# A decoder layer on one core: the first modulation loaded and computed by column halves, with v's first weights in between

## What is computed

```
sh1, sc1, ... = split(silu(c) @ w_ada + b_ada, 6)          # c: 9 rows (prompt and 8 samples), 1024 wide
h = x * rsqrt(mean(x*x) + eps) * norm1_g * (1 + sc1) + sh1
z = h @ w_in                                                # q, k, v, u, v (for the gating), gates
```

## Time and profile before

| | us |
|---|---|
| median of 3 runs | 1307.18 (1304.03 to 1307.71) |
| profiled execution, device time | 1306.45 |
| its span, first to last instruction | 1304.8 |
| PE busy in the span | 1230.2 (94%) |
| DVE, ACT, POOL busy | 659.8, 545.2, 195.6 |

### The profile page before, as it was taken

How to read it: one execution, slowest core, us unless ns; L and a number is a source line. 1 busy time by engine, 2 the same in 40 slices (tenths; PEclk the granted TensorE clock), 3 DMA queues, 4 the chain that set the end, 5 groups by cost and what they waited for, 6 DMA issues and landing times.

```text
span 1304.8 us, 17871 instructions
## 1 busy us (share of the span) xinstructions
PE 1230.2 (94%) x7112; PEld 926.7 (71%) x7112; DVE 659.8 (51%) x920; ACT 545.2 (42%) x866; POOL 195.6 (15%) x228
## 2 busy tenths in 40 slices
PE   4899999999999999998799999999989999999996
PEld 1677877777777887787667666747757888777762
DVE  1327613222161214123477551245677888888887
ACT  3723314011273135215334342202446787778752
POOL 1202200020000010001200020100044223222320
PEclk9899999999999999999799999999989999999999
DMA  9652311254443454538789995831389999999972
GB/s 355 212 213 68 102 65 65 65 173 180 144 168 100 148 190 163 173 129 319 262 296 383 383 343 185 269 103 35 115 302 305 371 375 380 373 369 376 370 292 92
DMA packets 126235, 293.96 MB, mean 225 GB/s; under 512 B 10160, under 2 KB 10288, under 8 KB 121496
## 3 DMA queue, kind: packets, MB, share of 16 engines
q1 hardware_dynamic: 108216, 243.57, 52.8%
q0 software_dynamic: 17952, 49.44, 10.7%
HBM read 269.91 MB, written 30.42 MB: 230 GB/s over the span
## 4 chain that ended last, share of the span: by engine, by line
PE 76%; DMA 13%; DVE 4%; ACT 3%; issue 2%; POOL 2%; SPq 0%; DVEq 0%; ACTq 0%; POOLq 0%
PE psum L1001 18%; PE psum L1003 17%; PE psum L1002 17%; PE psum L989 5%; PE psum L1043 5%; DMA arena<-in_cache_kv_w_dram 3%; DMA arena<-in_w_gate_dram 3%; PE psum L1374 2%; PE psum L1016 2%; PE psum L1282 2%; DMA arena<-in_w_ada_dram 2%; PE psum L1209 1%; DMA arena<-in_w_in_dram 1%; POOL slots_d L919 1%; DMA oscr<-arena 1%
## 5 line engine op out<-in xcount | busy, mean ns | idle before, releaser
L1001 PE MATMUL psum<-part,part 128*128 128x512 f32 (+1 forms) x1088 | 441.4, 406 | 11.3 <-DVE part L1960 5.0
L1002 PE MATMUL psum<-part,part 128*128 128x512 f32 (+1 forms) x1088 | 428.7, 394 | 0.0
L1003 PE MATMUL psum<-part,part 128*128 128x512 f32 (+1 forms) x1088 | 428.5, 394 | 0.0
L1001 PEld LDWEIGHTS psum<-part,part 128*128 128x128 f32 (+1 forms) x1088 | 219.4, 202 | 77.9 <-issue 21.8
L1003 PEld LDWEIGHTS psum<-part,part 128*128 128x128 f32 (+1 forms) x1088 | 219.3, 202 | 42.8
L1002 PEld LDWEIGHTS psum<-part,part 128*128 128x128 f32 (+1 forms) x1088 | 220.1, 202 | 38.0
L2378 DVE TENSOR_TENSOR part<-arena,part 128x2048 fp32r<-128x2048 f32 x96 | 218.4, 2289 | 33.7 <-ACT part L1810 32.3
L1909 DVE TENSOR_TENSOR part<-arena,part 128x2048 fp32r<-128x2048 f32 x42 | 96.4, 2300 | 251.0 <-PE psum L1043 224.7
L1810 ACT ACTIVATE part<-arena 128x2048 fp32r<-128x2048 f32 x94 | 179.2, 1920 | 36.9 <-DMA arena<-in_w_up_dram 17.0
L1578 ACT ACTIVATE arena<-psum 128x512 f32<-128x512 f32 (+3 forms) x128 | 73.6, 597 | 239.4 <-PE psum L1003 197.9
L1589 ACT ACTIVATE part<-arena 128x2048 fp32r<-128x2048 f32 x42 | 80.0, 1911 | 172.5 <-DMA arena<-in_w_in_dram 168.1
(11 more groups left out here) (289 smaller groups left out, 1075.8 us busy)
## 6 DMA issues: line engine op xcount, KB each, us to landing
arena<-in_w_in_dram SPq DMA_DIRECT2D x34, 1024.0 KB, 5.5
arena<-in_cache_kv_w_dram SPq DMA_DIRECT2D x16, 2048.0 KB, 12.2
arena<-in_w_gate_dram SPq DMA_DIRECT2D x32, 1024.0 KB, 10.0
arena<-in_w_up_dram SPq DMA_DIRECT2D x32, 1024.0 KB, 9.6
arena<-in_w_down_dram SPq DMA_DIRECT2D x32, 1024.0 KB, 10.0
arena<-in_w_ada_dram SPq DMA_DIRECT2D x24, 1024.0 KB, 7.7
arena<-in_cache_kv_w_dram SPq DMA_DIRECT2D x16, 1024.0 KB, 8.6
arena<-in_w_ada_final_dram SPq DMA_DIRECT2D x8, 1024.0 KB, 8.2
```

What stands on the lines that cost most here:

```text
L1001: nc.tensor.matmul(out_, hi, w_hi, start=start, stop=False)
L1002: nc.tensor.matmul(out_, hi, w_lo, start=False, stop=False)
L1003: last_product[0] = nc.tensor.matmul(out_, lo, w_hi, start=False, stop=stop)
```

## The change

The first modulation is cut by columns: half c has shift and scale of 512 features. A slot now holds two 1 MiB pieces (shift and scale columns of four groups k), so the whole modulation takes four slots, and v00 stands between the halves and v01 behind them. Groups 0 to 3 of h can be modulated with half 0 alone. PE computes half 1 (`first_step(1, d)`) inside v's first products. Even and odd groups k go to different column strips of the PSUM bank, so DVE adds two parts after the turn. x comes in two loads of 1 MiB and the samples' rows, each with its own semaphore. Of the constants only the identity (64 KB) is loaded at the start; the rest waits on POOL for v01.

```diff
-        put_ada(0, KD)
-        put_chunks("v", projected("v", 2), w_in, [QKV // CH + 2 + j for j in range(2)])
+        def put_first(c):
+
+            for s in range(2):
+                rows = w_ada[4 * P * s:4 * P * (s + 1), :].rearrange("(k p) n -> p k n", p=P)
+                put("ada0", [("ada", 4 * c + 2 * s + 1)],
+                    [(slice(4 * v, 4 * v + 4), rows[:, :, v * D + c * CH:v * D + (c + 1) * CH]) for v in range(2)])
+
+        v_chunk = [QKV // CH + 2 + j for j in range(2)]
+        for half in range(2):
+            put_first(half)
+            put("v", [projected("v", 2)[0][half]], halves(w_in, v_chunk[0])[half])
+            split[-1] = True
+        put_chunks("v", projected("v", 2)[1:], w_in, v_chunk[1:])
...
-            pool.dma_start(cst[:, :], t["consts"]).then_inc(const_in, 16)
+            pool.dma_start(c_("ident"), t["consts"][:, 0:P]).then_inc(ident_in, 16)
...
             pool.wait_ge(slot_in[S0["v"][1] % SLOTS], slot_total[S0["v"][1]])
+            pool.dma_start(cst[:, P:CONST_W], t["consts"][:, P:CONST_W]).then_inc(const_in, 16)
...
+            def first_step(c, d):
+
+                n = S0["ada0"][2 * c + d // 2]
+                slot_wait(n)
+                if c == 1 and d == 0:
+                    pe.wait_ge(mod_row, 1)
+                w = slot(n).rearrange("p (v k n) -> p v k n", v=2, k=4)
+                for v in range(2):
+                    for odd in range(2):
+                        at_ = 64 * v + 32 * odd
+                        ins = nc.tensor.matmul(ada_bank[at_:at_ + 32, :], cT[:, 2 * d + odd, :], w[:, v, 2 * (d % 2) + odd, :],
+                                               start=(d == 0), stop=(d == 3))
+                ins.then_inc(ada_read, 1)
...
-            for k in range(KD):
-                ada_step(0, k)
-                if k >= KD - TILES:
-                    i = k - (KD - TILES)
-                    pe.wait_ge(x_scaled, i + 1)
...
-            turn_rows(modrow)
...
+            first_step(0, 0)
+            first_step(0, 1)
+            for i in range(4):
+                turn_x(i)
+            first_step(0, 2)
+            first_step(0, 3)
+            turn_x(4)
+            turn_rows(0)
...
+                    pe.wait_ge(h_lo, 4 * half + k + 1)
                     for i in range(4):
                         rows = slice(i * P, (i + 1) * P)
-                        three_passes(mm.bank(bank_of("v", 0, i)), hT[:, k, rows], hT_lo[:, k, rows], w_hi[:, k, :],
-                                     w_lo[:, k, :], k == 0, False)
-
-            first_rows(S0["v"][0])
+                        three_passes(mm.bank(bank_of("v", 0, i)), hT[:, 4 * half + k, rows], hT_lo[:, 4 * half + k, rows],
+                                     w_hi[:, k, :], w_lo[:, k, :], half == 0 and k == 0, half == 1 and k == 3)
+                        if half == 1 and k == 3:
+                            tally(mm_filled)
+                    if half == 0 and k == 1:
+                        for d in range(4):
+                            first_step(1, d)
+                    if half == 0 and k == 2:
+                        turn_rows(1)
+
+            first_rows(0)
             pe.wait_ge(h4_lo_set, 1)
             half_product("v", H_PARTS, 0, 0, 0, 4)
-            pe.wait_ge(h_lo, KD)
-            for i in range(TILES):
-                if i == 4:
-                    samples_product("v", 1, h4_raw, 0)
-                half_product("v", H_PARTS, 0, 0, 1, i)
+            first_rows(1)
+            pe.wait_ge(h4_lo_set, 2)
+            samples_product("v", 1, h4_raw, 0)
+            half_product("v", H_PARTS, 0, 0, 1, 4)
             project("v", H_PARTS, 1, ahead=(("v", 1, h4_raw), ("u", 0, h4_raw)))
...
-            m = tp.first["mod"]
-            tp.wait_filled(dve, m)
-            turned = tp.bank(m).rearrange("p (q v n) -> p v q n", q=4, v=4)
...
+                own(V.tensor_copy(odd_rows, odd))
+                own(V.tensor_tensor(modT[:, :, ks, :], even, odd_rows, ALU.add))
+                V.scalar_tensor_tensor(out=modT[:, 1, ks, :], in0=modT[:, 1, ks, :], scalar=1.0,
+                                       in1=gainT[:, ks].unsqueeze(2).to_broadcast([P, 4, 9]), op0=ALU.add, op1=ALU.mult
+                                       ).then_inc(tp_dve, 1)
```

More of the change, by code:

```diff
@@ L284, in build @@
         h4_raw = at(HT0, KD, TOK)[:, :, SEQ:TOK]
-        h4, h4_lo = parts(KEPT0, KEPT0 + KD * NS, KD, NS)
+        h4 = [parts(KEPT0 + half * 4 * NS, KEPT0 + (KD + half * 4) * NS, 4, NS) for half in range(2)]
         mix = at(MIX0, TILES, D)
@@ L404, in build @@
         KV_OUTS = [4, 4 + 10, 4 + 10 + 10]
-        const_in, x_in, c_in = sem("const_in"), sem("x_in"), sem("c_in")
+        ident_in, const_in, c_in = sem("ident_in"), sem("const_in"), sem("c_in")
+        x_in = [sem(f"x_in{n}") for n in range(3)]
+        mod_row = sem("mod_row")
         slot_in = [sem(f"slot_in{i}") for i in range(SLOTS)]
@@ L1100, in _, with turn_x @@
             transposes(tp.first["c"], 1, KD, [gain_rows])
-            for k in range(KD):
-                ada_step(0, k)
-                if k >= KD - TILES:
-                    i = k - (KD - TILES)
-                    pe.wait_ge(x_scaled, i + 1)
-                    for half in range(2):
-                        transposes(tp.first["h"], 2 * i + half, ROWS[i],
-                                   [x0[0:ROWS[i], i, (4 * half + q) * P:(4 * half + q + 1) * P] for q in range(4)])
-            turn_rows(modrow)
+            def turn_x(i):
+                pe.wait_ge(x_scaled, i + 1)
+                for half in range(2):
+                    transposes(tp.first["h"], 2 * i + half, ROWS[i],
+                               [x0[0:ROWS[i], i, (4 * half + q) * P:(4 * half + q + 1) * P] for q in range(4)])
@@ L1110, in _, with first_rows @@
+            first_step(0, 0)
[6 more added lines that the diff above has]
+            turn_rows(0)
             H_PARTS = (hT, hT_lo)
-            def first_rows(n):
+            def first_rows(half):
+                n = S0["v"][half]
                 half_wait(n)
                 _, w_hi, w_lo = half_slot(n)
-                for i in range(4):
-                    mm.wait_empty(pe, bank_of("v", 0, i))
@@ L1622, in _ @@
             split_to(S0["v"][0])
[L1623 to L1630, removed]
+            for c in range(2):
+                tp.wait_emptied(act, tp.first["mod"] + c)
+                for k in range(4 * c, 4 * c + 4):
+                    x = h_raw[:, k, 0:SEQ]
+                    own(nc.scalar.activation(x, x, ACT.Identity, scale=modT[:, 1, k, 0:1], bias=modT[:, 0, k, 0:1]))
+                    nc.scalar.activation(hT[:, k, 0:SEQ], x, ACT.Copy).then_inc(h_hi, 1)
+                act.wait_ge(h4_set, c + 1)
+                nc.scalar.activation(h4[c][0], h4_raw[:, 4 * c:4 * c + 4, :], ACT.Copy).then_inc(h4_hi, 1)
+                if c == 0:
                     split_to(S0["v"][1])
@@ L1943, in _, with modulation_row, modulation_turned @@
             dve.wait_ge(bias_in, 64)
-            dve.wait_ge(ada_read, KD)
-            V.tensor_tensor(modrow, ada_bank, modbias, ALU.add).then_inc(ada_out, 1)
-            m = tp.first["mod"]
-            tp.wait_filled(dve, m)
-            turned = tp.bank(m).rearrange("p (q v n) -> p v q n", q=4, v=4)
[L1949 to L1954, removed]
+            def modulation_row(c):
+                dve.wait_ge(ada_read, 4 * (c + 1))
+                V.tensor_tensor(modrow, ada_bank, modbias[:, c, :], ALU.add).then_inc((mod_row, ada_out)[c], 1)
+            def modulation_turned(c):
+                m, ks = tp.first["mod"] + c, slice(4 * c, 4 * c + 4)
+                tp.wait_filled(dve, m)
+                even, odd = (tp.bank(m).rearrange("p (q v o n) -> p o v q n", q=4, v=2, o=2)[:, o, :, :, 0:9] for o in range(2))
+                own(V.tensor_copy(odd_rows, odd))
[3 more added lines that the diff above has]
+                                       ).then_inc(tp_dve, 1)
+            modulation_row(0)
+            modulation_turned(0)
             split_to(S0["v"][0])
```

62 lines of the change are left out of this document (39 added, 23 removed).

## The result

| | before, us | changed, us |
|---|---|---|
| median | 1307.45 (6 runs, 1304.03 to 1309.92) | 1319.81 (6 runs, 1317.95 to 1323.09) |
| profiled execution, device time | 1306.45 | 1321.37 |
| its span | 1304.8 | 1319.7 |
| PE busy in the span | 1230.2 (94%) | 1233.5 (93%) |
| DVE, ACT, POOL busy | 659.8, 545.2, 195.6 | 663.4, 543.7, 200.6 |

The change makes the kernel slower: the ratio is 1.0093, 95% interval 1.0076 to 1.011, which is 12.2 us (9.9 to 14.4) of 1307.45. The forecast was 1321, range 1313 to 1326.

What follows compares the result with a forecast made beforehand. PE was taken to bound the kernel, three quarters of the chain. The samples' product starting chunk 1 comes 12.7 us later, low clock adds 1.5: +14.2 on 1306.45 is 1320.7, median 0.7 above, so 1321; range 1313 to 1326.

Steps and rivals of the forecast that it cites:

- The loads at the start: Modulation, x and constants loading: smaller constants give 1.7 us, PE's first step at 18.8, v00 landed at 27.0.
- PE up to its first product: Modulation steps and turns of x on PE: first product of v at 35.5, 7.2 us earlier.
- What is added in PE's stream: Inside v's products: four modulation steps 4.1 us and second turn 0.5; the 108 products end at 66.2.
- T: Moment when tile 0 of v is complete and SP may issue v10: 64.2, before 60.78.
- v10: Load on SP's queue, issued only at T: lands at T + 6.1.
- v11: Load behind v10 on SP, sharing packet for packet with POOL's zeros: 7.3 us more, lands at T + 13.4.
- High part, table, gelu, handoffs: ACT after v11 lands: 1.9, 1.28, 0.60 and 0.1 us, so the samples' product starts at T + 17.3 = 81.5.
- The clock: PE after 15 us idle starts chunk 1 at its lower clock level: 1.5 us lost.
- No meeting with the zeros: Rival: SP's queue drains before POOL's zeros; samples' product at T + 12.1 = 76.3, time 1316; chance 0.20.
- v11 behind the zeros: Rival: v11 waits until POOL's zeros are through, landing at T + 19.4; time 1327.5; chance 0.08.
- The wait is hidden: Rival: v10 and v11 land before PE needs them, if T is before 56.7; 1304.6 or 1301; chance 0.04.
- Absorbed further on: Rival: loss is absorbed later in the kernel, where PE waits for DMA; about 1307 to 1310; chance 0.07.

Runs made afterwards that it cites:

- e6: Kernel before with only x in three loads and, of the constants, only the identity at the start: 1307.27 us, ratio 0.9992 (0.9969 to 1.0014).
- e8: Kernel before with one added wait, SP issuing v10 only when tile 0 of v is complete: 1316.85 us, ratio 1.0065.
- e2: Changed kernel with POOL's clearing of memory (the zeros) held back until v11 has landed: 1317.03 us, ratio 1.0057.
- e4: Changed kernel with other ring places for the first six loads, so v10 and v11 take slots of the modulation's half 1: 1305.13 us, ratio 0.9971.
- e5: As e4, with two of the four steps of the modulation's second half run before v's first product: 1302.72 us, ratio 0.9945.
- e1: Changed kernel with the gelus of v's four prompt tiles ahead of v10's and v11's high parts in ACT's list: 1310.57 us, ratio 1.0013.
- e7: Changed kernel with both halves of the modulation loaded ahead of v00 and v01: 1310.27 us, ratio 1.0025.
- e3: Changed kernel with both e1's order on ACT and e2's late zeros: 1311.54 us, ratio 1.0027.

## Why the prediction was right, step by step

- **What bounds the kernel.** The two dates chosen were enough: 11.8 of the difference are there at 80.6, 13.4 with the low clock behind it, and 12.6 still at 850.3.
- **The loads at the start.** PE's first step was put at 18.8 and came at 18.09. The gain from x and the constants was taken too small, 1.7: e6 has 2.8 against the trace before and 2.0 against e8's, so by 0.3 to 1.1. Of the 0.7, 0.3 were given back by two cold steps that took 3.64 us where I had 1.94 + 1.4 = 3.3.
- **PE up to its first product.** Turns of x at 1.3 a tile took 1.41 (24.86 to 26.27), with PE released by ACT's copies each time, as argued. First product: 35.5 forecast, 35.14 measured.
- **What is added in PE's stream.** 4.6 forecast, 4.8 measured: the last of the 108 products starts at 65.81 and ends 0.227 later, 30.9 us after the first, against 26.1 before. But the parts differ. The steps took 3.7 (from 42.49 + 0.227 to 46.38) where I had 4.1, the turn 0.4 (from 49.00 + 0.227 to 49.59) where I had 0.5; 0.65 are a term that I had at nothing, a longer low clock behind the first product (ten products and not seven). End: 66.2 forecast, 66.0 measured. T: 64.2 forecast, SP's issue at 64.19. That T came out to a hundredth is luck: less added work and an earlier first product (0.9 together) stand against the clock and small delays.
- **v10.** T + 6.1 forecast, 70.17 is T + 6.0. e2 shows 5.3 without the zeros.
- **v11.** T + 13.4 forecast, 76.66 is T + 12.5. Here is the one size that was off by nearly a microsecond. The mechanism was right, the queues share packet for packet: between 72 and 74 us (queue, packets, MB, share of the 16 engines) the trace has

```profile
q0 software_dynamic: 144, 0.52, 64.0%
q1 hardware_dynamic: 146, 0.29, 37.4%
```

  A pair took 2/145 = 0.0138 us and not 0.0154. The Trainium skill, DMA: Bandwidth & Descriptors, section on queues, rings and completion order, says that an engine serves its queues by turns, a whole packet each; this case's trace agrees here (146 to 144). The prediction set the 209 packets with none of SP's against that rule, and read the row wrongly. SP issued that load at 73.74, but its first packet moved only at 76.8, so from 74.5 to 76.5 it had none under way. All its packets then moved by 81.8 (kernel before, 76.8 to 81.8 us):

```profile
q1 hardware_dynamic: 528, 1.05, 54.9%
q0 software_dynamic: 50, 0.14, 8.4%
```

  A load that e4 issues at 70.34 has its first packet at 74.4, and then takes its turn beside the zeros (e4, 75.3 to 77.3 us):

```profile
q0 software_dynamic: 145, 0.53, 65.0%
q1 hardware_dynamic: 146, 0.30, 38.3%
```

  So the bound at T + 19.4, which rested on that row, was no real one for a load issued ahead of the zeros.
- **High part, table, gelu, handoffs.** T + 12.5 to 80.62 is 3.96, forecast 3.9.
- **The clock.** 1.5 forecast, 3.53 - 1.95 = 1.6 measured, at a granted 0.50.
- **The sum.** +14.2 forecast against the profiled execution, +14.9 measured (1321.37 - 1306.45); by medians +12.4. The dates moved by 11.8 + 1.6 = 13.4, where the sum had 12.7 + 1.5; v11's 0.9 is nearly all of that difference, since T was met. The profiled execution is 1.6 longer than the median and loses 1.5 behind the gating's product, so part of the nearness of 1321 to 1319.81 is the chance of one execution.
- **The rivals.** *No meeting with the zeros*: ruled out for this kernel by 146 to 144, and built as e2, where its date (76.3 forecast, 76.06 measured) was right. *v11 behind the zeros*: it wasn't, by the same 146 packets. *The wait is hidden*: its condition, T before 56.7, was not met (64.19); e4 is what the kernel does when nothing waits for T, 1305.1 where this rival had 1304.6. (Its 1301 stood for a first product at 32.0, which no run had; e5's 1302.7 comes from the steps and the clock.) *Absorbed further on*: 13.4 at the gating and 12.6 at `w_pa` say no.

The cause is shown from both sides: the wait put into the kernel before costs 8.5 us (e8), and taken out of the changed one it turns +12.2 into -3.8 (e4, by the ratios). That ACT's order carries most of it is shown by e1.

## What to carry to other kernels

When loads of a ring change their order, write down for each load whose slot it now takes and when that is read: here a load moved to the front gave its long-lived slot to the fourth load behind it. Then follow the in-order lists: what stands behind the late load on its queue, and what stands behind its first reader on that engine. The same start, some 8 us earlier, was worth -3.8 or +12.2 us by the places of six loads alone, so price the release of every slot before the gain at the start.

## What the runs showed of the hardware

- **Sharing by packets favours the long ones.** With both queues at work, w_in's load in 2 KB packets got 146 packets in 2 us beside 144 packets of 4 KB zeros, and 371 in 2 us when the zeros were held back (e2, 72 to 74 us). v11 took 6.5 us instead of 2.7 behind v10.
- **A late first packet behind a busy queue.** A load of SP's queue moved its first packet 1.0 us after its issue where POOL's queue was quiet (before at 60.78 and 89.47, changed at 64.19, e4 at 63.49, e5 at 60.40, e7 at 71.34). Where POOL's queue had the engines full it took 3.0 us (before, 73.74), 3.1 (e6, 71.60), 3.6 and 4.1 (e4, 44.09 and 70.34) and 3.9 (e5, 67.24). In e4 at 74.4 and in e5 the zeros were still going, and the two queues then moved packet for packet (145 to 146, and 142 to 142 in e5 from 72 to 74), so it wasn't the end of the zeros that let the load start; what it was is not shown.
- **The clock after a short idle.** After 1.84 us of idle v's products ran at a granted 1.00, after 4.37 us at 0.50; e5 owes about as much to this as to the steps that it moved. That work in the gap (two steps of the modulation from 31.27) kept the clock up is what the two runs suggest; it was not tried apart from moving the steps. How long the low clock lasts isn't fixed by the idle time before: after 4.99 us (before) seven products started at the slower pace, after 5.00 us (e8) fourteen, which is 1.5 us.
- **Not additive.** Counted from tile 0, holding back the zeros gained at the samples' product 4.5 us where v11 was waited for (changed to e2), and 0.2 where it wasn't (e1 to e3).
